# The roots of x ahead of the third chunk's sums, and the samples' w_down rows in single tiles

## The reference

```python
mod = silu(c) @ w_ada + b_ada                   # w_ada: 1024 x 6144; sh1, sc1, gt1, sh2, sc2, gt2
h   = rmsnorm(x, g_norm1) * (1 + sc1) + sh1     # rmsnorm: x * rsqrt(mean(x * x) + eps) * g
...                                             # h @ w_in, mLSTM, gated chunk MLP -> mix
x   = x + gt1 * (mix @ w_out)
h2  = rmsnorm(x, g_norm2) * (1 + sc2) + sh2
a, bb = split(h2 @ w_gate_up)                   # 2 x 2816 columns
x   = x + gt2 * ((silu(a) * bb) @ w_down)       # w_down: 2816 x 1024
y   = rmsnorm(x, g_final)
```

## Time and profile before

| | |
|---|---|
| three timed runs | 2432.53, 2434.53, 2437.93 us |
| median | 2434.53 us |
| the profiled execution | 2427.21 us, its span 2425.3 us |
| TensorE busy | 2367.1 us, 98% of the span |
| VectorE busy | 1429.5 us, 59% |
| ScalarE busy | 955.1 us, 39% |
| GpSimd busy | 226.4 us, 9% |
| DMA | 356 MB, mean 147 GB/s |

### The profile page before, as it was taken

One profiled execution on the slowest core, in us unless ns is written; L12 is line 12 of the kernel. 1 busy time (PEld: TensorE's weight loads), 2 busy tenths in 40 slices (PEclk: granted clock), 3 DMA queues, 4 the chain that ended last, 5 costly groups with the idle time before them and its releaser, 6 DMA issues.

```text
span 2425.3 us, 33170 instructions
## 1 busy us (share of the span) xinstructions
PE 2367.1 (98%) x11944; PEld 1924.0 (79%) x11944; DVE 1429.5 (59%) x2099; ACT 955.1 (39%) x1300; POOL 226.4 (9%) x219
## 2 busy tenths in 40 slices
PE   5999999999999999999999999999999999999998
PEld 3688877787888888888888888888888877888866
DVE  4758566668846654446854854445769755333476
ACT  2333322226544243335644333334656323233344
POOL 0022011110003100000002200000002400000002
PEclk8999999999999999999999999999999999999999
DMA  8832389767552223336543223334765322222476
GB/s 286 278 97 71 130 276 314 247 214 234 157 147 71 87 78 95 104 95 195 176 143 92 84 78 95 99 95 133 223 220 152 104 80 70 86 78 79 140 271 205
DMA packets 372057, 356.45 MB, mean 147 GB/s; under 512 B 13656, under 2 KB 305020, under 8 KB 371927
## 3 DMA queue, kind: packets, MB, share of 16 engines
q1 hardware_dynamic: 332116, 261.42, 36.0%
q0 software_dynamic: 15872, 58.74, 6.7%
q10 hardware_dynamic: 23956, 34.81, 4.3%
HBM read 323.78 MB, written 31.14 MB: 146 GB/s over the span
## 4 chain that ended last, share of the span: by engine, by line
PE 84%; DVE 6%; DMA 4%; issue 3%; ACT 1%; POOL 1%; ACTq 0%; DVEq 0%; SPq 0%; POOLq 0%
PE banks L2218 19%; PE banks L2220 19%; PE banks L2219 18%; PE banks L2310 4%; PE banks L2312 4%; PE banks L2311 4%; PE banks L2283 2%; PE banks L2284 2%; PE banks L2285 2%; PE banks L2098 1%; DMA raw<-wd_scratch 1%; DVE w_lo L1551 1%; DMA down_rows<-in_w_down_dram 1%; DMA stage<-in_w_ada_dram 1%; PE banks L2232 1%
## 5 line engine op out<-in xcount | busy, mean ns | idle before, releaser
L2218 PE MATMUL banks<-hT_hi,w_lo 128*128 128x512 f32 x2176 | 858.9, 395 | 3.9 <-DVE w_lo L1551 1.7
L2220 PE MATMUL banks<-hT_hi,w_hi 128*128 128x512 f32 x2176 | 847.7, 390 | 0.0
L2219 PE MATMUL banks<-hT_lo,w_hi 128*128 128x512 f32 x2176 | 847.4, 389 | 0.0
L1551 DVE TENSOR_TENSOR w_lo<-raw,w_hi 128x1024 fp32r<-128x1024 f32 x312 | 394.7, 1265 | 320.1 <-ACT w_hi L992 316.9
L2218 PEld LDWEIGHTS banks<-hT_hi,w_lo 128*128 128x128 f32 x2176 | 408.6, 188 | 100.4 <-issue 9.3
L2220 PEld LDWEIGHTS banks<-hT_hi,w_hi 128*128 128x128 f32 x2176 | 408.5, 188 | 86.5
L2219 PEld LDWEIGHTS banks<-hT_lo,w_hi 128*128 128x128 f32 x2176 | 408.9, 188 | 81.3
L992 ACT ACTIVATE w_hi<-raw 128x1024 fp32r<-128x1024 f32 x306 | 322.3, 1053 | 308.3 <-PE banks L2220 167.2
L2310 PE MATMUL banks<-w_lo,part 128*128 128x512 f32 x616 | 243.8, 396 | 3.2 <-DVE w_lo L1725 2.9
L2312 PE MATMUL banks<-w_hi,part 128*128 128x512 f32 x616 | 240.1, 390 | 0.0
L2311 PE MATMUL banks<-w_hi,part 128*128 128x512 f32 x616 | 239.8, 389 | 0.0
(11 more groups left out here) (370 smaller groups left out, 2290.6 us busy)
## 6 DMA issues: line engine op xcount, KB each, us to landing
raw<-in_w_gate_up_dram SPq DMA_DIRECT2D x176, 512.0 KB, 3.7
raw<-wd_scratch SPq DMA_DIRECT2D x140, 512.0 KB, 4.1
raw<-in_w_in_dram SPq DMA_DIRECT2D x96, 512.0 KB, 3.8
ada_stage<-in_w_ada_dram ACTq DMA_DIRECT2D x8, 2048.0 KB
raw<-in_w_out_dram SPq DMA_DIRECT2D x32, 512.0 KB, 3.5
in_stage<-in_w_in_dram ACTq DMA_DIRECT2D x6, 2048.0 KB
wd_tmp<-in_w_down_dram POOLq DMA_DIRECT2D x11, 1024.0 KB, 6.6
down_rows<-in_w_down_dram POOLq DMA_DIRECT2D x11, 1024.0 KB, 6.6
```

Of the source, the lines that this page charges most:

```text
L1551: ve.tensor_tensor(w_lo[:, s % 2], raw[:, s % 2], w_hi[:, s % 2].bitcast(F32), ALU.subtract).then_inc(lo_done.sem, 1)
L2218: mm(out, w_lo[:, slot, k, :], rhs_hi[:, r, :], start=start and n == 0, stop=False)
L2219: mm(out, w_hi[:, slot, k, :], rhs_lo[:, r, :], start=False, stop=False)
L2220: ins = mm(out, w_hi[:, slot, k, :], rhs_hi[:, r, :], start=False, stop=stop and last)
```

## The change

In the first stage VectorE makes means, diagonal and (through GpSimd) roots before `modulation(2)`, and `split_lo(0, 0)` comes behind `modulation(3)`. TensorE turns the tiles of x in another order: 0 and 2 before `thin(3)`, then 1 and 3, with a wait for `modulation(2)`, since tile 1 takes the bank that it reads. In the last block `down_rows` becomes three places of one tile; 22 loads of 512 KB go to them in turn, the first three at once, each later one when the tile before it in its place has been read. `state_out` comes behind the third load.

```diff
-        down_rows = place("down_rows", [P, 2, D], F32, HT)
+        down_rows = [place(f"down_rows{i}", [P, D], F32, at) for i, at in enumerate((HT, HT + 4 * kb, HL + 11 * kb))]
...
+        down_rows_in = [sem(f"down_rows_in{i}") for i in range(3)]
...
-                    for g in range(FT // 2):
-                        if g == 0:
+                    for k in range(FT):
+                        if k == 0:
                             pool.wait_ge(slab_used.sem, slab_used.at(blk, S_DOWN))
-                        else:
-                            pool.wait_ge(sem("s_read"), N_OUT + 2 * FT + g)
-                        pool.dma_start(down_rows[:, :, :], down_v[:, 2 * g:2 * g + 2, :])\
-                            .then_inc(sem("down_rows_in"), 16)
-                        if g == 0:
+                        elif k >= 3:
+                            pool.wait_ge(sem("s_read"), N_OUT + 2 * FT + (k - 3) // 2 + 1)
+                        pool.dma_start(down_rows[k % 3][:, :], down_v[:, k, :]).then_inc(down_rows_in[k % 3], 16)
+                        if k == 2:
                             state_out()
...
-            modulation(2)
             mean_square(0, -1)
             ve.tensor_tensor(dg[:, :, :], ident[:, :].unsqueeze(1).broadcast_to([P, TT, P]),
                              each_head(rrt[:, :]), ALU.mult).then_inc(sem("small_set"), 1)
+            modulation(2)
...
+            modulation(3)
             split_lo(0, 0)
-            modulation(3)
...
             pe.wait_ge(sem("small_set"), 2)
-            first_norm(range(2))
+            first_norm((0, 2))
             thin(3, hTs, R, BLK)
-            first_norm(range(2, 4))
+            pe.wait_ge(thin_ev.sem, thin_ev.at(0, N_ADA0 - 1))
+            first_norm((1, 3))
...
-                pe.wait_ge(sem("down_rows_in"), 16 * (g + 1))
+                for k in (2 * g, 2 * g + 1):
+                    pe.wait_ge(down_rows_in[k % 3], 16 * (k // 3 + 1))
```

More of the change, by code:

```diff
@@ L2263, in sample_down @@
                         at = GRP * (2 * k + j)
-                        ins = mm(SP_[at:at + GRP, :], s_actp[:, 2 * g + k, :], down_rows[:, k, j * BLK:(j + 1) * BLK],
+                        row = down_rows[(2 * g + k) % 3]
+                        ins = mm(SP_[at:at + GRP, :], s_actp[:, 2 * g + k, :], row[:, j * BLK:(j + 1) * BLK],
                                  start=g == 0, stop=g == FT // 2 - 1, tile_position=(0, at))
```

## The result

The changed kernel takes 2417.26 us (median of six runs, 2415.87 to 2420.05); the kernel before, run beside it and with the three runs shown, has a median of 2431.16. The ratio is **0.9941 [0.9929, 0.9953]**: faster, by 13.9 us. The profiled execution took 2416.63 us with a span of 2414.7, 10.6 less than the one before.

The account below looks back on a forecast made before the run. With TensorE busy 98% of the span, the change could pay only where TensorE waits or runs at its low clock. 6.0 (first stage) + 4.2 (last block) = 10.2 us off 2434.5 gave 2424.3 us, range 2417.5 to 2431.

Parts of the forecast that it names:

- rival A: Whole kernel: both parts of the change pay as forecast, 2424.3 us; chance 0.66.
- the base: Whole kernel: the gain is taken off 2434.53 us, the median of the timed runs of the kernel before.
- the clock in the first stage: First turns of x: clock rises in or near them, ending at 33.2, the middle; last four tiles stay at 5.40 us.
- the two upper bounds, 8.6 and 4.3: Most gain in us: first stage with full clock and no low stretch in the last tiles; last block with no down_rows wait.
- First stage, 6.0: Start of the kernel: earlier roots and dg end the last four tiles of x at 44.6 instead of 50.67, gaining 6.0 us.
- Rival C: First stage: the clock stays low through thin(3), gain 3.4 + 4.2 = 7.6 us, 2426.9; chance 0.10.
- The cover of ScalarE's queue: First stage: a later first norm tile is hidden, as the slab product wants it only 4.5 us after it starts; cost nothing.
- the slip of up to 1.3: First stage: ScalarE's first norm tile may start 1.3 us later, with half a megabyte more ahead of its DMA issues.
- Last block, 4.2: Last block: each read waits for only 0.5 MB of down_rows, so nearly all 4.33 us of waits go, gaining 4.2.
- B: Last block: half tiles land no earlier than whole ones, so only 6.0 us is gained, 2428.5; chance 0.13.
- D: Block 0: the first stage's gain is given back to w_ada loads or w_down scratch copies, 4.2 alone, 2430.3; chance 0.07.
- E: Last block: two engines' loads collide and TensorE waits for w_lo, 1.5 us in each of ten intervals, 2439.4; chance 0.04.

Follow-up runs that it names:

- e8: The changed kernel once more, no edit, on the same chip as three other follow-up runs: 2416.65 us, ratio 0.9938.
- e10: The changed kernel with split_lo(0, 0) ahead of modulation(3) again, as before: 2419.76 us, ratio 0.9942.
- e2: The kernel before with the first-stage part of the change alone, down_rows as it was: 2423.53 us, ratio 0.9975.
- e6: The changed kernel with two places of one tile for down_rows instead of three, still 22 loads: 2421.74 us, ratio 0.9967.
- e7: The changed kernel with ScalarE's issue of the sixth chunk of w_ada moved behind the eight norm tiles: 2416.82 us, ratio 0.9942.
- the twelve matmuls: Unused matmuls while TensorE waits for dg, in the kernel before (2430.66 us) and in the kernel with the last-block part alone (2422.32 us).
- e9: The changed kernel with tiles of x in the old order, 0 and 1 before thin(3), roots still early: 2420.64 us, ratio 0.9946.

## Why the prediction was right and wrong

The direction held, and both parts pay, as rival A has it. The size did not hold: 2417.26 is just under the range. 7.0 us lie between 2424.3 and 2417.26, of which 3.4 are in the base and 3.7 in the terms of the sum (10.2 forecast, 13.9 measured). The steps that failed are the base, the clock in the first stage, and the last block's term with its upper bound, both read from one profile.

- **The base.** "The gain is taken off the median": 2434.53, of three runs; beside the changed kernel it was 2431.16, and 2430.85 over 81 runs. For the profiled execution the sum gave 2417.0 and the profile after shows 2416.63. That is luck in part: the first stage gave 2.1 us more than its term, the last block 0.2 less, and the way between took 1.5, while the profiled execution of the kernel before was one of its quicker ones. The range's lower end took off 4 us for the spread and the two upper bounds, 8.6 and 4.3; the second of them was no bound, as the last block's item below shows. (2434.5 - 12.9 - 4 is 2417.6, where the prediction has 2417.5.)
- **First stage, 6.0.** The path was right: turns directly behind thin(2), no wait for `dg` in the profile after. Its start had less slack than the sum said, since `dg` was done at 29.66 and not 28.5; in e8 and e10, where thin(2) ended at 29.3 and 28.9, the turns waited 0.28 and 0.88 us for it. The gain was 8.1 us, near the upper bound of 8.6. The step that failed is the clock. The turned rows came at 36.63 instead of 38.1 (1.5 us), because thin(2) ended earlier and the first turns took 2.05 us where the middle of two clocks, 2.8, was taken. The last four tiles took 3.84 us where I let them keep their low stretch at 5.40 (1.6), and 0.77 were lost to the wait below. That makes the 2.3 us between 44.6 and 42.33. The low stretch went in five profiles with TensorE in the changed order (after, e2, e6, e7, e8) and came back in the sixth (e10). That the clock rises sooner without the pause is what the twelve matmuls show (first slab 3.4 to 3.7 us earlier); it does not keep the clock up in every execution. The Trainium skill (TensorE: Matmul & The Clock Gate, "What's actually happening") says that the window in which the clock gate watches TensorE is not reset when a kernel starts, and that the point of the rise varies with it. Two profiles of the changed kernel agree so far as the clock was up from 29.1 on in one and from 31.0 on in the other. Rival C, a low clock through thin(3), came true in part in one profile (thin(3) took 2.37 us in e10) and in none of the six others with early roots (1.9 each).
- **The cover of ScalarE's queue.** "Covered" was wrong by 0.77 us, the wait for `hT_lo`; the slip of up to 1.3 was rightly placed but compared with four tiles at 5.40, not 3.84.
- **Last block, 4.2.** 4.0 in the first pair of profiles, 5.8 timed alone, 7.1 between the means of all profiles. The mechanism held: a read waits for half a megabyte, since the other half was asked for one read earlier, and that half lands sooner. The half did not land in half the time, 4.2 us, but in 5.4 (median), mostly within the 6.6 that TensorE leaves it, so that the waits nearly went. What was mis-sized is how much there was to gain. The 4.3 us of one profile were taken for all there is; with one place the waits were 4.3, 5.0, 5.6 and 9.1 us in four profiles, and in three of them low stretches of the clock followed. The Trainium skill (DMA: Bandwidth & Descriptors, "Rules for kernel authors") asks for 1 MiB or more per DMA where the most bandwidth is wanted. Splitting alone gained nothing here (e6), which doesn't go against it. With a third place the kernel gained with 0.5 MB per DMA, since TensorE waited for one buffer's next tiles.
- **Rivals.** B fell: the half tiles that a read waits for do land earlier, and the gain is more than 6.0. D: the 1.5 us lost between first slab and last block in the first pair are within the spread of the twelve profiles. E: waits for `w_lo` in the last block were 2.9, 1.2, 0.9 and 0.3 us with one place and 0.9 to 4.1 with three; nothing like ten times 1.5.

What stays open: how much of the time is the clock's, and what decides in an execution whether the last four tiles get a low stretch.

## What to carry to other kernels

Before you take a gain off a measured time, ask how much that time spreads and how much of the spread is the very wait that you remove: the waits of one profile are one draw. When a buffer is loaded late, ask what the next read still waits for: a third place let half of it be asked for one read earlier, while splitting the load without a further place brought nothing. And when a pause of TensorE goes, look at the granted clock behind it, in more than one execution: the low stretch that followed went in five profiles out of six.

## What was not expected of the hardware

In the last block, waits of TensorE of 2.1, 2.2, 2.4 and 3.7 us between dense products were each followed by a stretch at 1.2 GHz (the read at 2401.99 took 1.94 for 1.07 us); one of 2.4 us, with the two places, was not, nor were those of 1.2 to 1.7 us in the earlier trace rows. The length of the wait alone does not tell: a wait of 1.58 us near 2010 us was followed by one in e7 and e9, while the like wait in the other ten profiles was not. In e7:

```profile
2011.62 0.50 PE L2219 MATMUL banks<-hT_hi,w_lo 128*128 128x512 f32 x1 [1.58 <-DVE hT_lo L1557]
```

```profile
2012.80:2016.20 3.40, 3.40 (x36) 2.17 (x36) 1.78 (x4) 1.79 (x2) 0.00 (x0) 0.50 0.00 0
```

Single low stretches also come between 78 and 91 us in five of the twelve profiles and between 1881 and 1893 us in six; neither the first profile of the kernel before nor that of the changed one has any of them.

Runs of kernels with one place or two for `down_rows` spread by 3.5 to 5 us (standard deviation), those with three places by 1.5 to 2.6. A DMA issue on ScalarE's queue held that engine for 3.73 us when three had gone in the 1.4 us before it, as 3.47 in the earlier trace rows.
